# A hybrid attention and expert-retrieval step: tile 4 ranked last, rows scored between the ranking steps, two finishes shared between engines

## What is computed

```python
def peer(x, w_query, sub_keys, expert_u, expert_v):
    q = (xt @ w_query).reshape(t, PEER_HEADS, 2, PEER_KEY_DIM // 2)
    s = jnp.einsum('thpd,hpkd->thpk', q, sub_keys).astype(jnp.float32)
    s_half, i_half = lax.top_k(s, PEER_TOPK)                      # 16 of 128, twice per head
    cand = s_half[:, :, 0, :, None] + s_half[:, :, 1, None, :]
    cand_idx = i_half[:, :, 0, :, None] * N_KEYS + i_half[:, :, 1, None, :]
    top_s, top_pos = lax.top_k(cand.reshape(...), PEER_TOPK)
    experts = jnp.take_along_axis(cand_idx.reshape(...), top_pos, axis=-1)
    gates = jax.nn.softmax(top_s, axis=-1)
    ...
    a = jax.nn.gelu(jnp.einsum('tkd,td->tk', expert_u[es], xs), approximate=False)
    return jnp.einsum('tk,tkd->td', gs * a, expert_v[es])

x = layer_norm(ALPHA * x + ga1 * (merged @ w_o), ln1_g, ln1_b)
u2 = x * (1 + sc2) + sh2
x = layer_norm(ALPHA * x + ga2 * peer(u2, ...), ln2_g, ln2_b)
```

## Time and profile before

| | us |
|---|---|
| median of 3 timed runs | 1932.91 |
| lowest, highest | 1929.52, 1939.39 |
| the profiled execution | 1945.27 |
| its span in the trace | 1943.5 |
| mean granted TensorE clock | 0.97 |
| TensorE busy | 1795.4 (92%) |
| VectorE busy | 1292.2 (66%) |
| GpSimd busy | 896.7 (46%) |
| ScalarE busy | 293.5 (15%) |
| moved by DMA | 670.21 MB, 345 GB/s |

### The profile page before, as it was taken

The page is one execution under the profiler, slowest core; times in us unless marked ns, Lnnn a source line. Parts: engine busy times, 40 slices in busy tenths (PEclk is TensorE's granted clock), DMA queues, the critical chain, the costliest instruction groups (busy, mean ns, idle before and its releaser), DMA issues.

```text
span 1943.5 us, 21544 instructions
## 1 busy us (share of the span) xinstructions
PE 1795.4 (92%) x8020; PEld 1152.3 (59%) x8020; DVE 1292.2 (66%) x2593; ACT 293.5 (15%) x661; POOL 896.7 (46%) x837
## 2 busy tenths in 40 slices
PE   4988898998999999998999999996889999999994
PEld 1666743554444359987888888884554444444441
DVE  2110476989579699998998975568875623336767
ACT  0120010555100001111111100005550000000000
POOL 1010225665456324334455555668865665435540
PEclk9999999999999999998999999998999999999998
DMA  8895859888999977559999999999989999999995
GB/s 360 338 370 214 344 160 394 291 286 324 392 324 363 390 272 298 187 192 362 366 361 375 386 387 409 405 394 329 327 308 409 409 409 409 409 409 409 409 410 203
DMA packets 168441, 670.21 MB, mean 345 GB/s; under 512 B 19563, under 2 KB 19691, under 8 KB 163085
## 3 DMA queue, kind: packets, MB, share of 16 engines
q0 software_dynamic: 112512, 410.79, 56.2%
q1 hardware_dynamic: 51072, 242.25, 31.8%
q10 hardware_dynamic: 4752, 15.81, 2.1%
HBM read 659.27 MB, written 7.39 MB: 343 GB/s over the span
## 4 chain that ended last, share of the span: by engine, by line
PE 46%; DMA 18%; DVE 18%; POOL 11%; issue 6%; ACT 1%; ACTq 0%; DVEq 0%; another core or an unknown queue 0%; POOLq 0%
PE psum L966 19%; POOL arena L566 11%; DMA arena<-in_expert_u_dram,arena 9%; DMA arena<-in_expert_v_dram,arena 4%; DVE arena L1511 4%; PE psum L751 4%; PE psum L992 3%; PE psum L995 3%; DVE psum L1784 3%; PE psum L740 2%; PE psum L1029 2%; DVE arena L1707 2%; DMA arena<-in_w_ada_dram 2%; PE psum L1006 2%; PE psum L1004 2%
## 5 line engine op out<-in xcount | busy, mean ns | idle before, releaser
L566 POOL DMA_INDIRECT arena<-in_expert_u_dram,arena x384 | 468.5, 1220 | 386.0 <-DVE arena L1511 261.6
L1511 DVE CUSTOM_DVE_ANT_0 arena<-arena 128x1024 f32<-128x1024 f32 x384 | 461.0, 1222 | 182.1 <-DMA arena<-in_expert_u_dram,arena 153.0
L566 POOL DMA_INDIRECT arena<-in_expert_v_dram,arena x384 | 390.7, 1018 | 357.9 <-DVE psum L1784 175.9
L1784 DVE SCALAR_TENSOR_TENSOR psum<-arena,psum 128x1024 f32<-128x1024 f32 x254 | 327.0, 1287 | 193.2 <-DMA arena<-in_expert_v_dram,arena 165.0
L893 PE MATMUL psum<-arena 128*128 128x256 f32 x2048 | 446.0, 381 | 7.3 <-DMA arena<-in_expert_uT_dram 7.3
L966 PE MATMUL psum<-arena 128*128 128x512 f32 x1024 | 443.7, 594 | 1.6 <-DMA arena<-in_expert_v_dram 1.6
L893 PEld LDWEIGHTS psum<-arena 128*128 128x128 f32 x2048 | 390.8, 191 | 61.3 <-issue 7.6
L966 PEld LDWEIGHTS psum<-arena 128*128 128x128 f32 x1024 | 193.3, 190 | 253.0 <-issue 249.0
L1064 PE MATMUL psum<-arena 128*128 128x128 f32 x1280 | 148.9, 278 | 2.1 <-DVE arena L1668 1.4
L1064 PEld LDWEIGHTS psum<-arena 128*128 128x128 f32 x1280 | 147.1, 194 | 3.6 <-issue 1.9
L1324 ACT ACTIVATE arena<-psum 128x512 f32<-128x512 f32 x64 | 38.2, 597 | 379.7 <-PE psum L893 292.6
(11 more groups left out here) (188 smaller groups left out, 1410.1 us busy)
## 6 DMA issues: line engine op xcount, KB each, us to landing
arena<-in_expert_uT_dram SPq DMA_DIRECT2D x128, 512.0 KB
arena<-in_expert_v_dram SPq DMA_DIRECT2D x128, 512.0 KB
arena<-in_w_ada_dram SPq DMA_DIRECT2D x12, 2048.0 KB
arena<-in_w_in_dram SPq DMA_DIRECT2D x11, 2048.0 KB
arena<-in_w_query_dram SPq DMA_DIRECT2D x8, 2048.0 KB, 22.7
arena<-in_w_in_dram SPq DMA_DIRECT2D x30, 512.0 KB, 7.9
arena<-in_w_o_dram SPq DMA_DIRECT2D x4, 2048.0 KB
arena<-in_expert_u_dram,arena POOLq DMA_INDIRECT x384
```

The source lines that it names most:

```text
L566: pool.indirect_dma_start(slot, None, table[0], bass.IndirectOffsetOnAxis(ap=number, axis=0)).then_inc(land, 16)
L1511: dve.tensor_tensor_reduce(UR[b], UR[b], U2B[e], 1.0, 0.0, ALU.mult, ALU.add, DOTS[e % 2][:, k:k + 1]).then_inc(u_free, 1)
L1784: dve.scalar_tensor_tensor(ys, row, weight, ys, ALU.mult, ALU.add).then_inc(v_free, 1)
```

## The change

`ORDER` becomes 0, 1, 3, 2, 4. In the loop of 30 steps, 10 to 19 are tile 2 now and 20 to 29 tile 4. `DOTS_AFTER` becomes a set of 25 steps with one group each, nearly every step from 0 on, and goes through the rows of tile 1 and then of tile 2; `SCORED_GROUPS` is 12, so 28 groups stand ahead of the gates and four groups of tile 2 behind them instead of six. `late_rounds` and `ROUND_AFTER` stay.

Buffers move with it. Tile 4's key scores lie in columns of `UT` that are free by then (`late_scores`); its digits and gate lie in `AF`, `BF` and `GATE[1]`, so its transposes (`spread`) wait until the weights of tile 1 were turned (`rank_out`), and come after the whole loop of `expert_scores`; VectorE waits for them ahead of its first one-hot tile, since `HOT_J[0]` now lies over the ranking's own buffers. `U2B[2]` takes the place of `U2B[1]`, so its load waits for the last dot of tile 1. The last 24 blocks of `expert_u` are taken in another order (`scored_block`), and the gelu waits for the routing of tile 4 at steps 48, 56 and 60, in place of waits for tile 2 at 28 and 52.

`SHARED` = (2, 3): of these finishes VectorE does the sums and the statistics, ScalarE the normalisation (`tail_normed`), GpSimd gain and shift (`tail_gain_shift`, behind all its fetches), and SyncE stores after it.

```diff
-ORDER = (0, 1, 3, 4, 2)
+ORDER = (0, 1, 3, 2, 4)
-        LATE = {e: at(o, 4, HALF) for e, o in ((1, 26624), (3, 35840), (4, 37888), (2, 39936))}
+        LATE = {e: at(o, 4, HALF) for e, o in ((1, 26624), (3, 37888), (2, 39936))}
-        U2B = [at(47104, D), at(44032, D), at(47104, D)]
+        U2B = [at(47104, D), at(44032, D), at(44032, D)]
-        HOT_J = [at(44032, BATCH, NKEYS), UT[:, :, 3 * P:4 * P]]
+        HOT_J = [at(47104, BATCH, NKEYS), UT[:, :, 3 * P:4 * P]]
+        def late_scores(e, qg):
+
+            if e == ORDER[-1]:
+                return UT[:, 2 * qg:2 * qg + 2, 0:2 * P]
+            return LATE[e][:, qg, :].rearrange("p (a b) -> p a b", a=2)
+
+        def scored_block(n):
+
+            i = n - KEYHALF - UPPER_PARTS
+            return n if i < 0 else KEYHALF + UPPER_PARTS + (i + 16) % 24
             def store_y(e):
-                sp.wait_ge(fin_step, FIN * (e + 1))
+                if e in SHARED:
+                    sp.wait_ge(tail_shifted, SHARED.index(e) + 1)
+                else:
+                    sp.wait_ge(fin_step, FIN_AT[e + 1])
+            def tail_gain_shift():
+
+                for i, e in enumerate(SHARED):
+                    pool.wait_ge(tail_normed, i + 1)
+                    pool.tensor_tensor(X1B[e], X1B[e], PRM2[1][1], ALU.mult).then_inc(tail_gained, 1)
+                    pool.wait_ge(tail_gained, i + 1)
+                    pool.tensor_tensor(X1B[e], X1B[e], PRM2[1][2], ALU.add).then_inc(tail_shifted, 1)
             routed(2)
+            score_rows(2, 0, GROUP)
+            pool.wait_ge(u_free, GROUP + 2 * HK)
             pool.dma_start(U2B[2], u2_d[2 * P:3 * P, :]).then_inc(late_u2_in, 16)
-            score_rows(2, 0, GROUP * SCORED_GROUPS)
+            score_rows(2, GROUP, GROUP * SCORED_GROUPS)
...
             last_values()
+            tail_gain_shift()
...
                 expert_scores(m)
+            spread(ORDER[-1])
             for i in range(BATCHES):
...
             def deviation(e):
-                act.wait_ge(fin_step, FIN * e + (8 if e == ENDING[-1] else 6))
+                act.wait_ge(fin_step, FIN_AT[e] + (8 if e == ENDING[-1] else 6))
                 act.activation(RSTD[:, 0:1], MV[:, 1:2], ACT.Sqrt).then_inc(fsqrt_done, 1)
+                if e in SHARED:
+                    act.wait_ge(fin_step, FIN_AT[e] + 8)
+                    act.activation(X1B[e], X1B[e], ACT.Identity, scale=RSTD[:, 1:2], bias=MV[:, 0:1]
+                                   ).then_inc(tail_normed, 1)
...
+                if m == (KEYHALF + UPPER_PARTS) // 2 + 4:
+                    act.wait_ge(pick_step, PICKED[4] - PICKS_OF[4] + ROUTE_AT[3])
+                if m == (KEYHALF + UPPER_PARTS) // 2 + 8:
+                    act.wait_ge(pick_step, PICKED[4] - PICKS_OF[4] + ROUTE_AT[5])
...
+                if e - 1 in SHARED:
+                    dve.wait_ge(tail_normed, SHARED.index(e - 1) + 1)
                 statistics(fin_step, base + 2, x1)
...
+                if e in SHARED:
+                    dve.wait_ge(fsqrt_done, e + 1)
+                    dve.reciprocal(RSTD[:, 1:2], RSTD[:, 0:1]).then_inc(fin_step, 1)
+                    dve.wait_ge(fin_step, FIN_AT[e] + 7)
+                    dve.scalar_tensor_tensor(MV[:, 0:1], MV[:, 0:1], -1.0, RSTD[:, 1:2], ALU.mult, ALU.mult
+                                             ).then_inc(fin_step, 1)
+                else:
+                    normed(fin_step, FIN_AT[e] + 2, X1B[e], prm[1], prm[2], fsqrt_done, e + 1)
...
+                if i == 0:
+                    dve.wait_ge(spread_done, len(DENSE))
...
+                for r in range(scored_rows[0], scored_rows[0] + count):
+                    if r == HK:
+                        dve.wait_ge(q_done, 4 * TILES)
+                        dve.memset(COLUMNS, 0.0).then_inc(zero_set, 1)
+                        dve.wait_ge(late_u2_in, 16)
+                    if r == HK + GROUP * WEIGH_AFTER:
+                        weigh(1)
+                    score(1 + r // HK, r % HK, r % HK + 1)
...
-DOTS_AFTER = {3: 1, 5: 1, 7: 1, 9: 1, 11: 1, 13: 1, 15: 1, 17: 1, 19: 1, 21: 1, 22: 1, 23: 1, 25: 1, 27: 1, 29: 1}
-FINISH_AT, DEVIATION_AT, STORE_AT = 9, 8, 32
+DOTS_AFTER = (0, 1, 2, 3, 5, 7, 9, 10, 11, 12, 13, 15, 16, 17, 18, 19, 20, 21, 22, 23, 24, 25, 26, 27, 28)
+FINISH_AT, DEVIATION_AT, STORE_AT = 3, 6, 32
-SCORED_GROUPS, GATE_ROUNDS = 10, 20
+SCORED_GROUPS, GATE_ROUNDS = 12, 20
```

More of the change, by code:

```diff
@@ L249, in backbone @@
         EID, GATE, DOTS = EID + [keep(HK).bitcast(U32)], GATE + [keep(HK)], DOTS + [keep(HK)]
-        DGATE = {e: at(4 * P + P * d, HK) for d, e in enumerate(DENSE)}
         FIRST = keep(GROUP)
@@ L1693, in rank_keys, with scored @@
                     dve.wait_ge(topk_step, 20 * si)
-                sc = LATE[e][:, qg, :] if e else bank(2 + si % 2)
+                def scored(c):
+                    if e:
+                        return late_scores(e, qg)[:, c // 2, c % 2 * P:(c % 2 + 1) * P]
+                    return bank(2 + si % 2)[:, c * P:(c + 1) * P]
                 def best(c, lo):
@@ L1701, in rank_keys @@
                     for c in range(4):
-                        src = sc[:, c * P:(c + 1) * P] if lo == 0 else SW[:, c, :]
+                        src = scored(c) if lo == 0 else SW[:, c, :]
                         dve.max(VAL[:, best(c, lo)], src).then_inc(topk_step, 1)
@@ L1873, in _, with score_next @@
             dve.wait_ge(u2_in, 16)
-            k = 0
-            for n, (do, e, part) in enumerate(
-                    [(rank_keys, 3, qg) for qg in range(4)] + [(route, 3, part) for part in range(PARTS)]
-                    + [(rank_keys, 4, qg) for qg in range(4)] + [(route, 4, part) for part in range(PARTS)]
-                    + [(rank_keys, 2, qg) for qg in range(4)] + [(route, 2, part) for part in range(PARTS)]):
+            scored_rows = [0]
+            def score_next(count):
+                for r in range(scored_rows[0], scored_rows[0] + count):
[6 more added lines that the diff above has]
+                    score(1 + r // HK, r % HK, r % HK + 1)
+                scored_rows[0] += count
+            steps = []
+            for e in ORDER[2:]:
+                steps += [(rank_keys, e, qg) for qg in range(4)] + [(route, e, part) for part in range(PARTS)]
+            for n, (do, e, part) in enumerate(steps):
                 do(e, part)
@@ L1906 @@
 FIN = 9
+SHARED = (2, 3)
+FIN_AT = [FIN * e - sum(a < e for a in SHARED) for e in range(TILES + 1)]
 SUB_AT = 3 + 5 * PEER_HEADS + 1
```

48 lines of the change are left out of this document (22 added, 26 removed).

## The result

The changed kernel takes 1941.78 us (median of 14 runs, 1938.71 to 1950.29), the kernel before 1931.21 us (14 runs, 1924.98 to 1940.65). The ratio is 1.0069, with a 95% interval from 1.0054 to 1.0083: 13 us slower by the ratio, 10.6 by the medians. The profiled execution took 1942.4 us with a span of 1940.6.

A forecast was written before the change was run, and what follows sets the result against it. Row fetches, not TensorE, were taken to bound the kernel at the stage borders. Order +14, value stage -2.6 and shared finishes -3.0 sum to +8.4 us on the 1932.9 median: 1941 us, own range 1932 to 1951, overall 1921 to 1957.

The forecast's parts named there:

- The order, up to the gates: Scoring stage: new order and two more groups ahead move the gates from 1323.74 to 1337, +14 us, bounds -10 to +33.
- Rounds: Scoring stage: one ranking step of 5.1 us plus one group of eight dots, taken as 17.6 us, ends 16.7 and 18.6.
- The signs named: Trace marks that would show the forecast right, such as last dot before gates near 1337 and TensorE idle some 24 us.
- The handover: Scoring, between tiles 1 and 2: U2B's load waits for tile 1's last dot, +8 us, bounds 0 to +8.8.
- The gelu's waits and `spread`: Scoring on TensorE: new routing waits cost nothing; the moved transposes take about 1 us, hidden while rows end later.
- The value stage: Two groups fewer save 33 us of fetching, mostly lost waiting for TensorE's round 20: -2.6 us, bounds 0 and -10.
- The shared finishes: End of program: passes leave VectorE for ScalarE and GpSimd; -3.4 for VectorE, counted as -3.0 us, bounds -3.4 and +2.
- the port: Rival, tail: as forecast, but GpSimd and VectorE stop each other, +3 to +5 us, 1945; chance 0.05.
- The gate stage: Dense gates between scoring and value stage: keeps its instructions, 0 us.
- The rounds at the fetch bound: Faster rival, scoring: steps cost nothing, rounds take 16.7 us, handover covered; total -13 us, 1920; chance 0.18.
- the rounds at 18.6: Slower rival, scoring: each step delays the buffers' refill, rounds take 18.6 us, +19 on top, 1960; chance 0.20.
- Nothing left: Rival, value stage and end: earlier rows are kept, -10 with earlier finishes gives back 13 against 14, 1934; chance 0.12.

The follow-up runs named there:

- the square above: Four kernels, ten or twelve groups ahead of the gates, rows dealt or not: first score to first one-hot tile 464.6, 490.4, 451.2 and 477.5 us.
- e3: The changed kernel without the load of tile 2's input and both waits on it, tile 2's scores left wrong: 1933.51 us, ratio to before 1.0002.
- e9: The changed kernel with TensorE's late rounds moved up and round 23's rows fetched ahead of the fifth to eighth value row: 1938.58 us, ratio to before 1.0033.
- e4: The changed kernel with SCORED_GROUPS 10 in place of 12: 1915.31 us, ratio to before 0.9925.
- e12: The changed kernel with ten groups ahead of the gates, the same program as e4 run once more: 1918.16 us, ratio to before 0.9921.
- e1: The kernel before, unchanged, run once more for a second profile: 1929.48 us, span 1927.7.
- e8: The changed kernel with ten groups ahead of the gates and no shared finishes: 1921.3 us, ratio to before 0.9940.
- e6: The kernel before with SCORED_GROUPS 12 in place of 10 and nothing else: 1954.66 us, ratio to before 1.0102.
- e2: The changed kernel, twelve groups, with the finishes of tiles 2 and 3 on VectorE alone: 1937.8 us, ratio to before 1.0029.
- e10: The changed kernel with ten groups ahead of the gates and only tile 2's finish shared: 1916.1 us, ratio to before 0.9922.

## Why the prediction was right, step by step

The forecast was 1941 us, in a range from 1921 to 1957; 1941.78 was measured. It was made on the median, so that the late beginning of the profiled execution fell out of it; had the sum been put on that execution's own time, it would have said 1953.7. That it is met within 1 us is luck: the sum of +8.4 stands against +12.9 in the profiles and 10.6 between the medians, and its base of 1932.9, a median of three runs, lay 1.7 us above the 1931.2 of fourteen.

**The order, up to the gates: right.** +14 forecast (1337 less 1323.74 is 13.3), +12.9 measured between marks counted from the first score, 13.3 from the first fetch. The forecast's own 1337 - 859.2 = 477.8 us stands against 477.5, but that is partly chance: counted from the first fetch it is 500.4 against 493.2, since the rounds were cheaper than taken. Rounds were put at 17.6 with ends of 16.7 and 18.6, and are 17.4 and 17.0. The last three groups came out at 12.8 us instead of 12; the prediction's own terms (4 x 1.24 + 6.5 + 1.2) make 12.7. The first dot came 4.3 us behind its fetch and the eighth 5.9 behind its own (841.38 to 847.30), not some 7. The signs named were off in absolute time (the first dot at 835.8 for 845, tile 1's last at 1123 for 1135, the last before the gates at 1324.6 for 1337): the fetches began 5.1 us earlier than in the profile that was read (831.46 for 836.58), and the rest is a landing and rounds that cost less than taken. TensorE's idle time ahead of the gates, forecast at 24 us, is 28.7: its own end, at 1298.4, came 15.6 us earlier than the 1314 taken and the first one-hot tile 12.4, and the 2.5 us from that tile to the first gate matmul stood in no term.

The sum hid a fact, though. It went through the rounds one by one and never set the dealing and the two groups against each other; the square above shows that the dealing alone was worth 13 us, and that the forecast of a slower kernel rests wholly on the two groups.

**The handover: right in kind, somewhat small in size.** 8 us taken, with 8.8 as the end; VectorE waits 10.61, and e3 gives 8.3 to 10.1 back. The load took 11.8 us, as in the earlier trace rows, and was issued 5.0 us behind the last dot; less the 6 us of cover that makes the 10.6. The round came out at 26.0 us (taken: 25.5), 8.6 above the 17.4 of its neighbours.

**The gelu's waits and `spread`: right**, nothing lay on them.

**The value stage: right in mechanism.** -2.6 forecast, -4.3 measured, inside the bounds. GpSimd runs dry and restarts at 1571.27 (forecast: the same 1572.66) and VectorE's next row follows at 1585.3 (forecast 1581.3). The size was misread: the 1584 that the forecast gives this row before the change stands in none of its rows. The trace that was read has it at 1591.17, behind the four fetches of round 22, so both ends of the -2.6 were too early, and the lead counted from the first value matmul is 4.8 us. The stretch below 409 GB/s is there as described. The 33 us of fetching saved became 32.7 us more of waiting (35.8 against 3.1).

**The shared finishes: wrong, in sign too.** -3.0 with bounds of -3.4 and +2; measured +2.2. The term for VectorE failed because two of its operations stand still beside GpSimd, 1.3 and 1.5 us; that was the rival named the port, priced at +3 to +5, and it has to be added to the forecast rather than to stand for itself. The rule cited from the Trainium skill (SBUF — State Buffer, section "SBUF: two separate sides") agrees with the rows above: the operations that stood still (L1781, L1812) have two inputs in SBUF; the one with an input in PSUM (1.22 us) and the one with a single input (0.16 us) weren't touched. It was weighed against one operation of VectorE and met two. The other part, GpSimd's 9.3 us of closing stretch behind its last pass, stood in no term and no rival: no row of before showed GpSimd working late enough to see it.

**The rest.** The gate stage was put at 0 and reads +2.1, which is within what it varies. The steps' errors are -1, +2, -2 and +5 us, +4.5 in all: they cancel in part, and the base's 1.7 us and the spread of the runs cover the rest. So the mechanism is borne out up to the value stage, but the closeness of the total tells nothing of the tail.

**The rivals.** The rounds at the fetch bound did not come: rounds of 17.0 to 17.4 lie between the 16.7 of that rival and the 17.6 taken, but the handover wasn't covered. Nor did the rounds at 18.6. "Nothing left" was priced at -10 for the value stage; e9 shows 4 us of it, with the obstacle (the buffers that come free at step 36) that wasn't seen in the code.

## What to carry to other kernels

When a change mixes several parts, work out each part's price alone as well as their sum: here ten groups with the new order run in 1915 to 1918 us, 0.8% faster than before (0.9925, 0.9900 to 0.9949), and the whole change is 0.7% slower; the two differ in one constant, `SCORED_GROUPS`. Work that is moved ahead of a barrier on which an engine already stands idle costs its full length there; look first whether the place that it leaves can use the room, or only waits at the next fixed point. An engine that was done early may have a long closing stretch that nobody has seen: before handing it the last work of a program, count that stretch into the end.

## What the runs showed of the hardware

- The drain that closes GpSimd's program ends 2.0 to 2.6 us behind its last tensor operation in four of the programs here and 9.3 us behind it in four others (e4 and e12, two executions of one program, both show 2.6). With only row fetches left before it, it ended at 1918.6 in the profile read for the prediction, 29 us behind the last fetch and 1.7 us after the last row had landed (1.7 in e1 and e8 too, 5.1 in e6 and e2). What sets its length wasn't found.
- An operation of VectorE on a single column (0.16 us) took 1.48 us when it began amid a GpSimd pass of 2.34 us over SBUF, one of 512 columns 2.21 instead of some 0.7 (L1812, the first of its pair), one of 1024 columns 3.10 instead of 1.28 (e10). The price of the meeting was about the rest of GpSimd's instruction in all three, whatever VectorE's own size.
- Gathers of 4 KB rows and the dense stream together moved 409 to 410 GB/s in each stretch of 25 us and more of e4's value stage from 1450 to 1880, with this one core at work. The Trainium skill (DMA: Bandwidth & Descriptors, section "Where 436 GB/s comes from") says that about 358 GB/s, a core's half of its memory's rate, bind transfers from HBM and that 435 is the ceiling of the fabric; here the trace stands above the first figure and below the second.
